# A two-layer transformer block kernel: its first parameters, first norm sums, and the place where the norm is applied

## What is computed

```python
def first_block(x, positions, g_pre_mix, w_in, ssm_lambda_re, ssm_lambda_im, ssm_log_dt, ...):
    hn = rms_norm(h, g_pre_mix[l])
    proj = hn @ w_in[l]
    u = proj[..., :SSM_WIDTH]                       # 512 columns: state space mixer
    q = proj[..., SSM_WIDTH:SSM_WIDTH + ATTN_WIDTH] # 512
    k, v = ...                                      # 128 and 128
    y_ssm = s5_mixer(u, lam_re, lam_im, log_dt, ...)
    q = partial_rotary(q, positions); k = partial_rotary(k, positions)
    y_attn = sliding_window_sink_attention(q, k, v, attn_sinks[l])
    merged = concat([rms_norm(y_ssm, g_ssm_out[l]), rms_norm(y_attn, g_attn_out[l])])
    h = h + rms_norm(merged @ w_out[l], g_post_mix[l])
    ... gated feed-forward; the second block follows
```

## Time and profile before

| | us |
|---|---|
| three runs: lowest, median, highest | 2356.20, 2364.24, 8599.52 |
| the profiled execution, its own time | 2353.87 |
| span inside it, first to last instruction | 2352.0 |
| time outside the span | 1.87 |

### The profile page before, as it was taken

The page is one execution under the profiler, slowest core; times in us unless marked ns, Lnnn a source line. Parts: engine busy times, 40 slices in busy tenths (PEclk is TensorE's granted clock), DMA queues, the critical chain, the costliest instruction groups (busy, mean ns, idle before and its releaser), DMA issues.

```text
span 2352.0 us, 29837 instructions
## 1 busy us (share of the span) xinstructions
PE 2193.4 (93%) x11134; PEld 1795.0 (76%) x11134; DVE 1278.7 (54%) x1993; ACT 901.6 (38%) x1299; POOL 91.5 (4%) x99
## 2 busy tenths in 40 slices
PE   7858899999998999999997899999999978999997
PEld 6735778888876888888875788888777867888886
DVE  6965454434445566655565743244568876433444
ACT  4224332322225556555642432232244424422422
POOL 1000120000040000000000000000000000000000
PEclk9979899999999999999998999999899989999998
DMA  4001213232132222222211222232112212232221
GB/s 160 29 10 37 89 54 107 77 105 105 69 110 81 81 85 69 80 72 85 76 67 39 76 101 90 91 105 90 63 63 72 71 55 72 89 99 98 89 90 54
DMA packets 32091, 185.54 MB, mean 79 GB/s; under 512 B 4736, under 2 KB 5120, under 8 KB 13312
## 3 DMA queue, kind: packets, MB, share of 16 engines
q1 hardware_dynamic: 27216, 176.17, 21.7%
q10 hardware_dynamic: 2736, 6.00, 0.7%
q0 software_dynamic: 2048, 2.17, 0.4%
HBM read 180.06 MB, written 2.10 MB: 77 GB/s over the span
## 4 chain that ended last, share of the span: by engine, by line
PE 82%; DVE 10%; DVEq 4%; ACT 2%; issue 2%; ACTq 0%; DMA 0%; POOL 0%; POOLq 0%
PE ps L517 12%; PE ps L518 12%; PE ps L519 12%; PE ps L908 5%; PE ps L910 5%; PE ps L909 5%; PE ps L950 3%; PE ps L951 3%; PE ps L952 3%; PE ps L540 2%; PE ps L579 2%; PE ps L542 2%; PE ps L541 2%; DVE f_run L2245 1%; PE ps L846 1%
## 5 line engine op out<-in xcount | busy, mean ns | idle before, releaser
L1084 ACT ACTIVATE w_hi<-raw 128x2048 fp32r<-128x2048 f32 x122 | 232.8, 1908 | 298.0 <-PE ps L519 217.0
L517 PE MATMUL ps<-x_hi,w_lo 128*128 128x512 f32 x864 | 336.9, 390 | 5.8 <-DVE w_lo L1481 3.6
L519 PE MATMUL ps<-x_hi,w_hi 128*128 128x512 f32 x864 | 336.2, 389 | 0.0
L518 PE MATMUL ps<-x_lo,w_hi 128*128 128x512 f32 x864 | 336.2, 389 | 0.0
L1481 DVE TENSOR_TENSOR w_lo<-raw,w_hi 128x2048 fp32r<-128x2048 f32 x122 | 280.0, 2295 | 83.3 <-ACT w_hi L1084 82.9
L908 PE MATMUL ps<-x_hi,w_lo 128*128 128x512 f32 x560 | 225.2, 402 | 6.3 <-DVE w_lo L2061 6.3
L910 PE MATMUL ps<-x_hi,w_hi 128*128 128x512 f32 x560 | 219.6, 392 | 0.0
L909 PE MATMUL ps<-x_lo,w_hi 128*128 128x512 f32 x560 | 218.5, 390 | 0.0
L517 PEld LDWEIGHTS ps<-x_hi,w_lo 128*128 128x128 f32 x864 | 162.2, 188 | 41.5 <-DVE w_lo L1481 4.5
L519 PEld LDWEIGHTS ps<-x_hi,w_hi 128*128 128x128 f32 x864 | 162.2, 188 | 33.8
L518 PEld LDWEIGHTS ps<-x_lo,w_hi 128*128 128x128 f32 x864 | 162.2, 188 | 33.2
(11 more groups left out here) (403 smaller groups left out, 4020.0 us busy)
## 6 DMA issues: line engine op xcount, KB each, us to landing
raw<-w_attn_in SPq DMA_DIRECT2D x32, 1024.0 KB, 4.9
raw<-w_gate_up SPq DMA_DIRECT2D x22, 1024.0 KB, 4.9
raw<-w_up_a SPq DMA_DIRECT2D x16, 1024.0 KB, 4.9
raw<-w_down_a SPq DMA_DIRECT2D x16, 1024.0 KB, 4.9
raw<-w_up_h SPq DMA_DIRECT2D x16, 1024.0 KB, 4.9
raw<-w_down_h SPq DMA_DIRECT2D x16, 1024.0 KB, 4.8
raw<-w_hgrn_in SPq DMA_DIRECT2D x8, 1024.0 KB, 4.9
raw<-w_down SPq DMA_DIRECT2D x8, 768.0 KB, 4.3
```

The source lines that it names most:

```text
L517: pe.matmul(o, w_lo[:, slot, a:a + P], hi[:, k, :], start=k == 0, stop=False)
L518: pe.matmul(o, w_hi[:, slot, a:a + P], lo[:, k, :], start=False, stop=False)
L519: last = pe.matmul(o, w_hi[:, slot, a:a + P], hi[:, k, :], start=False, stop=k == st.kc - 1)
L1084: act.activation(w_hi[:, slot, :], raw[:, slot, :], ACT.Copy).then_inc(whi_ready, 1)
```

## The change

1. The small loads are put in two sets. ScalarE's queue carries only `lam`, `freq`, `pos` (semaphore `early_ready`) and `gains`, in this order. `consts` and the other six go to SP's queue, behind slab 1.
2. VectorE starts with a wait for `early_ready` and the first eight operations of the state space numbers, then `w_lo` of slab 0, then the eight `x_lo` with the rest of the numbers between them; `w_lo` of slab 1 follows the numbers.
3. TensorE no longer adds the squares inside slab 0. All eight sums stand behind it.
4. `q`, `k` and `v` tiles are taken out by ScalarE with plain copies (semaphore `qkv_taken`). VectorE multiplies the rotary tables by the norm instead, and ScalarE scales `v` by token when it copies the transposed tile.
5. A split is only as wide as the widest slab that its slot receives next (`next_width`).

```diff
+U_TILES = 4
...
-        free[s.reader] += s.tiles
+        free[s.reader] += U_TILES if name == "w_in" else s.tiles
...
+            def load_small():
+                sp.dma_start(consts[:, :, :], const_in).then_inc(consts_ready, 16)
+                small = [(iota, iota_in), (bc, bc_in), (c_re, c_in[:, 0]), (c_im, c_in[:, 1]), (mask_raw, mask_in),
+                         (sink, sink_in)]
...
                         if st.slab0 + c == 0:
                             load_x()
+                        if st.slab0 + c == 1:
+                            load_small()
...
                     if t >= len(W_IN_BANKS):
-                        pe.wait_ge(tile_free["dve"], t + 1 - len(W_IN_BANKS))
+                        before = t - len(W_IN_BANKS)
+                        if before < U_TILES:
+                            pe.wait_ge(tile_free["dve"], before + 1)
+                        else:
+                            pe.wait_ge(qkv_taken, before - U_TILES + 1)
...
+            st = STAGES["w_in"]
+            first_slab(st, None, xlo_ready, XB["w_in"])
             pe.wait_ge(consts_ready, 16)
-            st = STAGES["w_in"]
-            first_slab(st, None, xlo_ready, XB["w_in"], lambda k: sum_chunk("pre_mix", DC, k))
+            feature_sum("pre_mix", DC)
...
-            small = [(lam, lam_in), (sink, sink_in), (freq, freq_in),
-                     (pos, pos_in), (iota, iota_in), (bc, bc_in), (c_re, c_in[:, 0]), (c_im, c_in[:, 1]),
-                     (mask_raw, mask_in)]
-            assert len(small) == SMALL
+            early = [(lam, lam_in), (freq, freq_in), (pos, pos_in)]
+            assert len(early) == EARLY
+            for dst, src in early:
+                dst = dst[:, :, :] if len(dst.shape) == 3 else dst[:, :]
+                act.dma_start(dst, src).then_inc(early_ready, 16)
             act.dma_start(gains[:, :], gains_in).then_inc(gains_ready, 16)
...
-                act.activation(w_hi[:, slot, :], raw[:, slot, :], ACT.Copy).then_inc(whi_ready, 1)
+                width = next_width(st, c)
+                act.activation(w_hi[:, slot, 0:width], raw[:, slot, 0:width], ACT.Copy).then_inc(whi_ready, 1)
...
+            def take(t):
+                act.wait_ge(tile_done, t + 1)
+                act.activation(places[t - U_TILES], ps[:, W_IN_BANKS[t % len(W_IN_BANKS)], :], ACT.Copy) \
+                   .then_inc(qkv_taken, 1)
...
             act.wait_ge(vt1_done, 1)
-            act.activation(v1_tok[:, :, :].rearrange("p a c -> p (a c)"), ps[:, 2, :], ACT.Copy).then_inc(vt1_ready, 1)
+            act.wait_ge(rstd_ready, SK_ROOT["pre_mix"] + 1)
+            for b in range(TB):
+                last = act.activation(v1_tok[:, b, :], ps[:, 2, b * P:(b + 1) * P], ACT.Copy, scale=rstd4[:, b:b + 1])
+            last.then_inc(vt1_ready, 1)
...
+            dve.wait_ge(early_ready, 16 * EARLY)
+            ts(col("lr"), lam[:, 0, :], -1e-4, None, ALU.min)
+            exp_reduce(lam[:, 2, :])
             dve.wait_ge(whi_ready, 1)
             tt(w_lo[:, 0, :], raw[:, 0, :], w_hi[:, 0, :].bitcast(f32), ALU.subtract).then_inc(wlo_ready, 1)
             dve.wait_ge(gains_ready, 16)
...
+            tokens_lo(0)
+            exp_series(720.0, 120.0, 24.0)
+            tokens_lo(1)
...
+            dve.wait_ge(small_ready, 16 * SMALL)
             angles_begin()
             keep_rstd("pre_mix")
...
             input_powers()
-            take(4)
-            take(5)
             split_lo(st, 3, 0)
...
+            tt(rope_s[:, :], rope_s[:, :], rstd[:, :], ALU.mult)
+            tt(rope_c[:, :], rope_c[:, :], rstd[:, :], ALU.mult)
+            settle()
             dve.wait_ge(kr1_swap, 1)
```

More of the change, by code:

```diff
@@ L403, in joins, with widest, next_width @@
         return j == 3 and not (isinstance(p, int) and p == 1)
+    def widest(st):
+        return max(st.body) * st.kc * P
+    def next_width(st, c):
+        own = c < len(st.body) - 1 or st.trips > 1
+        after = [s for s in STAGES.values() if s.before is st] if c == len(st.body) - 1 else []
+        return max([widest(st)] * own + [widest(s) for s in after])
     def first(i):
@@ L429, in load_x @@
                       .then_inc(x_ready[half], 16)
+            def load_small():
+                sp.dma_start(consts[:, :, :], const_in).then_inc(consts_ready, 16)
+                small = [(iota, iota_in), (bc, bc_in), (c_re, c_in[:, 0]), (c_im, c_in[:, 1]), (mask_raw, mask_in),
+                         (sink, sink_in)]
+                assert len(small) == SMALL
+                for dst, src in small:
+                    dst = dst[:, :, :] if len(dst.shape) == 3 else dst[:, :]
+                    sp.dma_start(dst, src).then_inc(small_ready, 16)
             for name, st in STAGES.items():
@@ L684, in _ @@
             pe.wait_ge(lw_ready, 2 * STEP)
-            pe.wait_ge(tile_free["dve"], STAGES["w_in"].tiles - 2)
+            pe.wait_ge(tile_free["dve"], U_TILES)
+            pe.wait_ge(qkv_taken, 4)
             ssm_in(0)
@@ L1133, in _ @@
             act.activation(masks[:, :], mask_raw[:, :], ACT.Copy)
+            act.wait_ge(consts_ready, 16)
             act.activation(ident_b[:, :], ident, ACT.Copy).then_inc(mask_ready, 1)
+            places = [q1[:, c, :] for c in range(4)] + [k1[:, :], v1[:, :]]
+            def take(t):
+                act.wait_ge(tile_done, t + 1)
+                act.activation(places[t - U_TILES], ps[:, W_IN_BANKS[t % len(W_IN_BANKS)], :], ACT.Copy) \
+                   .then_inc(qkv_taken, 1)
             split_hi(w_in, 2, 0)
@@ L1138, in _ @@
             split_hi(w_in, 3, 0)
+            take(4)
+            take(5)
             split_hi(w_in, 4, 0)
+            take(6)
+            take(7)
             for j in range(STEP):
@@ L1144, in _ @@
                                    ACT.Copy, scale=sign).then_inc(lw_ready, 1)
+            take(8)
+            take(9)
             act.wait_ge(kt_zero, 1)
@@ L1504, in _, with exp_reduce @@
             last.then_inc(eps_ready, 1)
-            dve.wait_ge(whi_ready, 1)
-            tt(w_lo[:, 0, :], raw[:, 0, :], w_hi[:, 0, :].bitcast(f32), ALU.subtract).then_inc(wlo_ready, 1)
-            dve.wait_ge(gains_ready, 16)
-            for c in range(DC):
-                part_lo_gain("w_in", c, x_raw[:, c, :], gain("g_pre_mix", c))
-            split_lo(STAGES["w_in"], 0, 0)
-            dve.wait_ge(small_ready, 16 * SMALL)
             def col(name):
                 return par[:, PR[name], :]
-            def exp_parts(z):
+            def exp_reduce(z):
                 ts(col("z"), z, -87.0, 88.0, ALU.max, ALU.min)
@@ L1541, in reduce_turns, with tokens_lo @@
                 settle()
+            def tokens_lo(c):
+                part_lo_gain("w_in", c, x_raw[:, c, :], gain("g_pre_mix", c))
             li = lam[:, 1, :]
+            dve.wait_ge(early_ready, 16 * EARLY)
             ts(col("lr"), lam[:, 0, :], -1e-4, None, ALU.min)
-            exp_parts(lam[:, 2, :])
+            exp_reduce(lam[:, 2, :])
+            dve.wait_ge(whi_ready, 1)
+            tt(w_lo[:, 0, :], raw[:, 0, :], w_hi[:, 0, :].bitcast(f32), ALU.subtract).then_inc(wlo_ready, 1)
+            dve.wait_ge(gains_ready, 16)
+            tokens_lo(0)
+            exp_series(720.0, 120.0, 24.0)
+            tokens_lo(1)
+            exp_series(6.0, 2.0, 1.0)
+            settle()
             stt(col("dt"), col("e"), 1.0, col("two_k"), ALU.add, ALU.mult)
             settle()
+            tokens_lo(2)
             tt(col("t0"), col("lr"), col("dt"), ALU.mult)
@@ L1572, in _ @@
             settle()
+            tokens_lo(7)
             reduce_turns(col("r_lo"), col("r_hi"), 0)
-            ts(col("r_lo"), col("r_lo"), float(1 / TWO_PI), None, ALU.mult).then_inc(turn_ready, 1)
+            ts(col("r_lo"), col("r_lo"), float(1 / TWO_PI), None, ALU.mult)
+            split_lo(STAGES["w_in"], 0, 0)
             dve.tensor_copy(tmp[:, 1, :], pos[:, :])
@@ L1710, in _ @@
             st = STAGES["w_in"]
-            places = [q1[:, c, :] for c in range(4)] + [k1[:, :], v1[:, :]]
             def take(t):
```

37 lines of the change are left out of this document (20 added, 17 removed).

## The result

The changed kernel takes 2369.04 us (median of 20 executions, 2358.15 to 2372.65) where the kernel before takes 2356.37 (median of 20; 19 of them lie between 2348.12 and 2370.02, one far outside at 8599.52). The ratio is 1.0042, 95% interval [1.0026, 1.0058]: about 10 us slower, clear of zero and well inside 2%, where 2.9 us were forecast.

The account below looks back on a forecast made before the run. It took the time of VectorE's reciprocal and PE's pace to decide the first part; +1.6 us to slab 4 and +1.3 for the rotary tables, +2.9 on 2353.87, gave 2356.8 us, range 2346 to 2370.

Parts of the forecast that it names:

- Landings and the start of VectorE: Kernel start: pos lands at 12.5, gains about 15.2, first matmul 2.4 us late at 17.2, reciprocal unchanged at 44.7.
- Rival (b): Kernel start: small loads land with slab 0 near 6.9, reciprocal 5.4 us earlier, about 4.5 kept, 2352.3; chance 0.08.
- Slab 0: First slab of w_in: clock rises within 3.4 to 7.3 us, PE catches up with the supply and ends at 31.9.
- Rival (c): Low clock stays through slab 0 and the sums; spread ends at 56.6 instead of about 47.1, 2363.9; chance 0.12.
- The row of sums: Eight sums behind slab 0: 6.4 us plus 3 us for a falling clock, ending at 41.3.
- PE is now ahead and waits for the reciprocal: At the spread: PE arrives between 40.4 and 45.2, reciprocal at 44.7; the 6 us won end as a wait.
- From the spread to slab 4: Spread as late as before, cold rest of slab 1 loses 2.5 us, 0.76 us wait goes: net +1.6 us.
- The rotary tables: Between last x_lo and k step on VectorE: two multiplications of 0.68 each, 1.3 us with the drain, on the path.
- The unforeseen case: Something unseen, such as clock changes that fall elsewhere in the later stages; chance 0.10.
- slightly slower: Sign expected for the whole run, within the range: +2.9 us, 2356.8; within 2% at 0.98.
- ScalarE's takes, v's pieces, narrower splits at nothing: ScalarE's six copies nothing, at worst 0.6 us; v's four pieces 0, hidden by waiting; narrower splits 0, bound -2.2.

Follow-up runs that it names:

- e6: Kernel before plus two unused multiplications of the tables' size and their settling ahead of the first rotary step; 2369.05 us, ratio 1.0062.
- e9: Kernel before with 12 spare matmuls in TensorE's wait ahead of the q step and 10 in each of the two behind; 2352.07 us, ratio 0.9994.
- e15: Kernel before with two spare multiplications and their settling ahead of the second demodulation, in the state space stage; 2368.25 us, ratio 1.0043.
- e2: Changed kernel with q, k, v taken by VectorE again, rotary tables unscaled, v copied in one piece; 2352.53 us, ratio 0.9991.
- e8: e2 with 12 and 2 x 10 spare matmuls filling TensorE's waits at the q steps; 2349.99 us, ratio 0.9979.
- e3: Kernel before with only the eight sums moved behind slab 0; 2361.46 us, ratio 1.0022.
- e1: Changed kernel with the sums back between the chunks of slab 0; 2363.19 us, ratio 1.0037.
- e5: Changed kernel with the two rotary table multiplications moved behind VectorE's output matrix, where it waited 4.87 us; 2357.67 us, ratio 1.0012.
- e12: Kernel before with only the q, k, v part, tables scaled behind the output matrix, TensorE's waits filled (12 and 2 x 10); 2353.40 us, ratio 1.0007.
- e10: Changed kernel with tables scaled behind the output matrix and TensorE's waits filled with 12 and 2 x 10 spare matmuls; 2358.84 us, ratio 1.0031.
- e11: e8 with more filling, 20 and 2 x 16 spare matmuls; 2357.66 us, ratio 1.0029.
- e14: Kernel before with e6's two multiplications and their settling twice; 2361.18 us, ratio 1.0036.

## Why the prediction was wrong, point by point

- **Landings and the start of VectorE: right.** `pos` was put at 12.5 and came at 12.9, `gains` at 15.2 and 15.7; `w_lo` 14.2 and 14.42; first matmul 17.2 and 17.51; reciprocal 44.7 and 45.16. Rival (b), an early landing, fell. It named the rule of the Trainium skill ("DMA: Bandwidth & Descriptors", section on queues, rings and completion order) that a DMA engine drains a whole packet of one queue before it switches. The four landings some 3 us apart don't contradict that rule; they contradict what the rival took from it. All four in one turn would have landed together, while one load in each turn, with SP's large loads between, would look as it does here. No run tested this.
- **Slab 0: right.** The clock rose between 21.06 and 21.37, under 3.9 us after the first matmul (said: 3.4 to 7.3), and the slab ended at 32.1 (said: 31.9). Rival (c), the low clock all through, fell. In all eight traces with the sums behind the slab the clock rose 3.0 to 6.0 us after the first matmul; with the sums between it took from 5.4 us (e6) to 22.8 (before, e9, e15).
- **The row of sums: mis-sized.** Taken as 6.4 + 3 us, it took 11.0 here, since the clock was at the low level for more of it (0.62 in the mean). Other executions differ: the same row took from 8.7 us (e2) to 10.8 (e8) in the seven other traces that have it. With the nine matmuls cold too, 4.0 us, TensorE came to the spread at 47.10 instead of 40.4 to 45.2, behind the reciprocal and not ahead of it. "PE is now ahead and waits for the reciprocal" didn't happen in this execution; in e2 it did, for 0.70 us, and in e3 for 5.52.
- **From the spread to slab 4: the right size by two errors.** The norm's row was 1.5 us later (48.87 against 47.38), where no delay was expected; but the 2.5 us for a cold rest of slab 1 didn't come, because the clock rose at 48.6, with the spread itself. The takes on ScalarE gave 0.6 us, where 0.8 were forecast. Together +0.9 at the scans, where +1.6 was forecast, and +2.5 at the first rotary step, where the whole sum was +2.9: up to there the forecast was near, in part by luck. e1 confirms that this is small: with the sums back, the ratio is within the change's interval.
- **The rotary tables: the step that failed.** "1.3 us with the drain, on the path" is the length (1.35 measured), and the sum took it at that. Alone on the kernel before (e6) it costs 1.0062, 14.6 us. Put at another place (e15) it costs 1.0043, and hidden in a wait (e5) 1.0012 with an interval that covers 1: what costs is the delay and not the operation. The term should not have been a length alone but a length and what the clock does in the next stage. The attention had been costed at nothing because nothing in it was changed; 11.1 of the 17.0 us are there.
- **The unforeseen case** was named, "clock changes that fall elsewhere in the later stages", with a part of 0.10. The earlier trace rows already showed a clock of 0.77 ahead of it and the earlier trace rows falls at two later places. Those rows were used for how the clock rises again, and not for how much of the later program is at the mercy of it. The range to 2370 was wide enough, but for rival (c) and the spread between runs and not for this, so that the time fell inside it by luck; the direction, slightly slower, was right, and the middle was not.
- **ScalarE's takes, v's pieces, narrower splits at nothing: right as far as seen** (e5 and e12 have the takes and v's pieces and no cost clear of zero; e10 has them too and stands at 1.0031, which no part explains).

## What to carry to other kernels

A stage whose engine alternates between work and short waits can have a time that depends on where the clock's low stretches fall in it, and an edit that only delays it can cost several times its own length, as here. New operations are better put where their engine waits anyway, even when they are short (e5; e10 warns that this isn't certain). Before a small gain or loss is believed, measure a kernel that has only the delay (e6) or the same delay at another place (e15), over ten executions or more: one trace shows one of several lengths. And test a remedy on the kernel before as well: filling the wait looked like the cure on two kernels and did nothing on the others.

## What was not expected of the hardware

- TensorE's clock can fall behind a wait of 1.95 us or not: of the two such waits of the attention, both, one or none were followed by the low level, in 7, 3 and 7 traces of nearly the same instructions, and the three sizes go with it. The length of the wait ahead of it all didn't decide: 0.70 us (e11) came with 120.08 us of attention, 5.62 us (e14) with 113.87.
- During sixty-four one-column matmuls in a row the clock fell although TensorE was busy for all of their 11.01 us (0.62 in the mean); spread between wide matmuls, from 37.01 to 44.16 in before, they left it high (1.00 in the earlier trace rows).
- A load of 0.5 KB took 8.3 us to land as the second of its queue, one of 24 KB 5.1 us as the first and 10.8 as the third.
